# The passage from the FFN's up products to its down products: h loaded by quarters, the first down additions placed between the last pair's pieces

## What is computed

```
a, bb = jnp.split(u2 @ w_gate_upffn[i], 2, axis=-1)      # up: width 1024 -> 2 x 2816
h = h + (jax.nn.silu(a) * bb) @ w_down[i]                # down: 2816 -> 1024, added to h
```

## Time and profile before

| | before |
|---|---|
| median of 3 runs | 1698.7 us (1698.27 to 1705.17) |
| the profiled execution's own time | 1701.96 us |
| its span in the trace | 1700.2 us |
| PE busy | 1642.6 us, 97% of the span |
| DVE, POOL, ACT busy | 1157.0, 710.7, 624.9 us |
| bytes moved by DMA | 190.24 MB, mean 112 GB/s |

### The profile page before, as it was taken

How to read it: one execution, slowest core, us unless ns; L and a number is a source line. 1 busy time by engine, 2 the same in 40 slices (tenths; PEclk the granted TensorE clock), 3 DMA queues, 4 the chain that set the end, 5 groups by cost and what they waited for, 6 DMA issues and landing times.

```text
span 1700.2 us, 21565 instructions
## 1 busy us (share of the span) xinstructions
PE 1642.6 (97%) x7810; PEld 1353.8 (80%) x7810; DVE 1157.0 (68%) x1689; ACT 624.9 (37%) x978; POOL 710.7 (42%) x388
## 2 busy tenths in 40 slices
PE   9999999999999999999998999999989999989996
PEld 6888887887877888888886888878768888889785
DVE  7241799962498777777768666887948982585457
ACT  5031233421254444444443222264551111277114
POOL 2434111154514233223326687743465554443451
PEclk9999999999999999999999999999999999999998
DMA  5511100122523443344368976142101111100102
GB/s 192 84 45 42 36 27 29 35 102 109 185 88 125 174 155 141 144 163 152 146 229 311 408 311 260 70 155 58 36 25 50 49 49 38 63 26 1 37 26 99
DMA packets 52421, 190.24 MB, mean 112 GB/s; under 512 B 5681, under 2 KB 7618, under 8 KB 51562
## 3 DMA queue, kind: packets, MB, share of 16 engines
q1 hardware_dynamic: 47362, 171.61, 27.9%
q10 hardware_dynamic: 4968, 17.44, 3.5%
HBM read 133.97 MB, written 55.05 MB: 111 GB/s over the span
## 4 chain that ended last, share of the span: by engine, by line
PE 76%; DVE 12%; DMA 5%; issue 3%; ACT 2%; POOL 1%; ACTq 0%; POOLq 0%; SPq 0%; DVEq 0%
PE G L753 30%; PE U L996 10%; PE G L996 10%; PE U L1034 6%; PE G L1034 6%; PE G L1070 4%; DMA bias_scratch<-fvec 3%; PE U L1244 2%; PE U L899 1%; PE G L1231 1%; DMA h<-in_x_t 1%; DVE B_lo L1880 1%; DVE qt L1953 1%; DMA hid_spill<-hst 1%; DVE X_lo L2147 1%
## 5 line engine op out<-in xcount | busy, mean ns | idle before, releaser
L583 POOL TENSOR_SCALAR w_hi<-raw 128x1024 fp32r<-128x1024 f32 x50 | 149.6, 2991 | 295.1 <-PE G L753 217.8
L753 PE MATMUL G<-B_hi,w_hi 128*128 128x512 f32 x512 | 160.7, 395 | 5.0 <-DVE B_lo L1880 2.3
L753 PE MATMUL G<-B_lo,w_hi 128*128 128x512 f32 x512 | 158.4, 391 | 0.0
L753 PE MATMUL G<-B_hi,w_lo 128*128 128x512 f32 x512 | 158.0, 390 | 0.0
L753 PE MATMUL G<-A_hi,w_hi 128*128 128x512 f32 x448 | 144.3, 403 | 0.0
L621 POOL TENSOR_TENSOR S<-fraw 128x512 f32<-128x512 f32 x33 | 46.6, 1412 | 227.4 <-DVE ring_lo L2152 196.1
L753 PE MATMUL G<-A_lo,w_hi 128*128 128x512 f32 x448 | 138.9, 391 | 0.0
L753 PE MATMUL G<-A_hi,w_lo 128*128 128x512 f32 x448 | 138.3, 390 | 0.0
L585 POOL TENSOR_TENSOR w_lo<-raw,w_hi 128x1024 fp32r<-128x1024 f32 x50 | 132.2, 2645 | 4.2
L996 PE MATMUL G<-X_hi,ring_hi 128*128 128x512 f32 x308 | 120.7, 392 | 5.0 <-DVE X_lo L2147 2.9
L1469 ACT ACTIVATE ring_hi<-S 128x512 fp32r<-128x512 f32 x132 | 82.2, 628 | 110.2 <-PE U L1034 61.4
(11 more groups left out here) (393 smaller groups left out, 3841.2 us busy)
## 6 DMA issues: line engine op xcount, KB each, us to landing
raw<-in_weights SPq DMA_DIRECT2D x72, 512.0 KB, 3.6
hid_spill<-hst SPq DMA_DIRECT2D x72, 512.0 KB, 2.6
fraw<-in_weights SPq DMA_DIRECT2D x66, 512.0 KB, 4.5
Dc<-hid_spill SPq DMA_DIRECT2D x56, 512.0 KB, 12.5
Dc<-hid_spill ACTq DMA_DIRECT2D x14, 512.0 KB, 8.2
h<-in_x_t SPq DMA_DIRECT2D x8, 512.0 KB, 7.6
h<-in_x_t ACTq DMA_DIRECT2D x1, 4096.0 KB, 14.1
h_spill<-h SPq DMA_DIRECT2D x8, 512.0 KB, 6.7
```

The costliest lines, as they stand in the source:

```text
L583: pool.tensor_scalar(hi, raw[:, u, :], 1.0, None, ALU.mult).then_inc(w_hi_done, 1)
L753: mm = pe.matmul(G[g][:, b * HT:(b + 1) * HT], w, x[:, k, b * HT:(b + 1) * HT], start=s0, stop=s1)
```

## The change

1. **h by quarters.** `h_in(j)` becomes `h_in(j, *quarters)`. A quarter (a, n) is the tiles 4j + a and 4j + 2 + a, columns of half n: 512 KB in runs of 2 KB, where the whole load had runs of 16 KB. Each half of h has three semaphores: for (0, 0), for (1, 1), and one for (0, 1) and (1, 0) together. `down_add` waits for them at r = 0, 2 and 4 of the first two steps.
2. **SP's order.** The quarter (0, 0) of tiles 0 to 3 is issued after the first gated quarter of the last pair, (1, 1) after the second, the other two after the fourth. The quarter (0, 0) of tiles 4 to 7 is issued after the last pair's third piece, the other three after its seventh.
3. **DVE's order.** The additions of the first down step, which came after all four `turn_h`, with three of the pieces between them, are placed among the `turn_h` and the pieces: r = 0 after the first `turn_h`, r = 1 after the first piece, and so on.
4. **ACT's order.** The roundings of the weights UP + 1, r = 0 to 3, come after the fourth of the last pair's seven `hidden_hi` instead of after the seventh.

```diff
@@ SP
-            def h_in(j):
-                sp.dma_start(h[:, 4 * j:4 * j + 4, :].rearrange("p k n -> p (k n)"),
-                             h_spill[:, 4 * j * T:4 * (j + 1) * T]).then_inc(h_back[j], 16)
+            def h_in(j, *quarters):
+
+                for a, n in quarters:
+                    e = (0, 2, 1)[a + n]
+                    src = h_spill[:, 4 * j * T:4 * (j + 1) * T].rearrange("p (m a n) -> p m a n", m=2, a=2)
+                    dst = h[:, 4 * j:4 * j + 4, :].rearrange("p (m a) n -> p m a n", m=2)
+                    sp.dma_start(dst[:, :, a, hs(n)], src[:, :, a, hs(n)]).then_inc(h_back[j][e], 16)
...
+            sp.wait_ge(h_out, 16 * KT)
+            sp.wait_ge(hm_done, 4 * (GROUPS - 1) + 1)
+            h_in(0, (0, 0))
+            sp.wait_ge(hm_done, 4 * (GROUPS - 1) + 2)
+            h_in(0, (1, 1))
             sp.wait_ge(hm_done, 4 * GROUPS)
-            sp.wait_ge(h_out, 16 * KT)
-            h_in(0)
+            h_in(0, (0, 1), (1, 0))
             last += NR
-            for j in range(NR):
+            for j in range(3):
                 hidden_out(last + j)
-            for u in range(2):
-                sp.wait_ge(hs_out[u], 16 * (last // 2 + 1))
-            h_in(1)
+            sp.wait_ge(hs_out[0], 16 * (last // 2 + 1))
+            h_in(1, (0, 0))
+            for j in range(3, NR):
+                hidden_out(last + j)
+            sp.wait_ge(hs_out[1], 16 * (last // 2 + 1))
+            h_in(1, (1, 1), (0, 1), (1, 0))
             raw_in(UP + 2)
@@ ACT
-            for j in range(NR):
+            for j in range(4):
+                hidden_hi(last + j)
+            for r in range(4):
+                weights_hi(UP + 1, r)
+            for j in range(4, NR):
                 hidden_hi(last + j)
             for w in range(UP, LAST):
-                for r in range(NR):
+                for r in range(4 if w == UP else 0, NR):
                     weights_hi(w + 1, r)
@@ DVE
+                if d < 2 and r in (0, 2, 4):
+                    dve.wait_ge(h_back[d][r // 2], 32 if r == 4 else 16)
...
-            turn_h(last, 0), hidden_lo(NR * last), turn_h(last, 1), hidden_lo(NR * last + 1), turn_h(last, 2)
-            hidden_lo(NR * last + 2), hidden_lo(NR * last + 3), turn_h(last, 3)
-            dve.wait_ge(h_back[0], 16)
-            for r in range(NR):
+
+            def first_down(r):
                 down_add(r, 0, UP, 0, 0)
-                if r < 3:
-                    hidden_lo(NR * last + 4 + r)
-            dve.wait_ge(h_back[1], 16)
+            turn_h(last, 0), first_down(0)
+            hidden_lo(NR * last), first_down(1)
+            turn_h(last, 1), first_down(2)
+            hidden_lo(NR * last + 1), first_down(3)
+            turn_h(last, 2), hidden_lo(NR * last + 2), hidden_lo(NR * last + 3)
+            first_down(4)
+            turn_h(last, 3)
+            for j in range(4, NR):
+                hidden_lo(NR * last + j)
+            first_down(5), first_down(6)
```

More of the change, by code:

```diff
@@ L357, in build @@
         ch_in = [tile_in[0:NR], [sem(f"ch_in1_{r}") for r in range(NR)]]
-        h_back = [sem(f"h_back{j}") for j in range(2)]
+        h_back = [[sem(f"h_back{j}_{e}") for e in range(3)] for j in range(2)]
         dn_mid, dn_ev = sem("dn_mid"), [sem(f"dn_ev{m}") for m in range(2)]
```

## The result

| | before | after |
|---|---|---|
| median | 1698.2 us (1695.77 to 1705.17, 20 runs) | 1702.24 us (1698.29 to 1706.49, 20 runs) |
| ratio | | 1.0018, 95% interval 1.0009 to 1.0026: 3.1 us slower (1.5 to 4.4); the two medians differ by 4.0 |
| span of the profiled execution | 1700.2 us | 1697.8 us |
| PE's first down product starts | 909.16 us | 904.89 us |
| the stretch (below) | 85.05 us | 86.94 us |

The account below looks back on a forecast made before the run. PE, busy 97% of the span, was taken as the bound. Its 8.9 us stall goes, but the stream, 4.3 us late, starts step 4 3.0 us later: 1698.7 + 3.0 = 1701.7 us, range 1695.0 to 1706.0.

Parts of the forecast that it names:

- PE's stall at step 0: First down step, PE waiting for DVE's addition to h: 5.96 us plus 2.92 of slow clock, 8.9 us to win.
- the weights' stream: Saturated DMA transfers from about 933 to 1007 us: 4.3 us later than before, bounds 2.2 and 6.2.
- the slack: Start of down step 4: before the change, its weights' low part is ready 1.25 us ahead of PE's need.
- DVE's count: DVE's order in the first down step: 1.70 us per difference or piece beside POOL, 1.2 per pair of additions.
- the wait of 3.1 us at the start of step 1: PE waits 3.1 us for DVE's addition of r = 4, from 928.2 to 931.3.
- the slow clock behind it: After PE's earlier waits: a clock loss there only makes a later wait shorter.
- the forecast wait at step 3: Start of down step 3: PE ready at 973.9, low part at 976.8, a wait of 2.9 us.
- The estimate that I drew from it: DVE's last pieces: if each waits for one POOL operation, the seventh ends near 936, time 1.4 us above forecast.
- The seventh piece: Last of DVE's pieces, gating SP's later transfers: ends at 934.6 instead of 930.7, bounds 932.5 and 936.5.
- Two edits priced at nothing: ACT's earlier roundings of UP + 1: gain 0, bounds 0 to 1 us; early quarters of tiles 0 to 3: no gain.
- The gain did not arrive: Rival: the stream does not hold step 4, PE keeps 5.8 us, time 1692.9; chance 0.13.
- it did not even out: Rival: seventh piece ends before 932, stream late by no more than 1.25 us, time 1698.7; chance 0.12.
- the quarters did not run at half rate: Rival: quarters of tiles 4 to 7 hold DMA twice as long, 3.5 us on top, up to 1707.2; chance 0.05.

Follow-up runs that it names:

- the dose: Four extra 512 KB memory-to-memory copies issued ahead of the weights UP + 2: ratio to before 1.0049 in the changed kernel, 1.0026 in the kernel before.
- small_late: Changed kernel with ACT's three small loads for the second block (644 KB) issued two steps later; ratio to the kernel before 1.0010.
- h1_whole: Changed kernel with h of tiles 4 to 7 loaded in one 2 MB transfer behind the seventh piece instead of quarters; ratio to before 1.0017.
- wf_old_act: The kernel where the stream has been cleared, with ACT's order of the kernel before; ratio to the kernel before 0.9981.
- the kernel where the stream has been cleared: Changed kernel with weights UP + 2 to UP + 4 issued earlier by SP and ACT's three small loads later; ratio to the kernel before 0.9939.
- weights_first: Changed kernel with SP's order alone altered, weights UP + 2, UP + 3 and UP + 4 issued earlier; ratio to the kernel before 0.9978.
- wfsl_h0_late: The kernel where the stream has been cleared, with all quarters of h for tiles 0 to 3 issued behind the fourth gated quarter; ratio to before 0.9980.
- before_dose: Kernel before with four extra 512 KB copies between h of tiles 4 to 7 and the weights UP + 2; ratio to before 1.0026.
- before_weights_first: Kernel before with SP's order alone altered, weights UP + 2, UP + 3 and UP + 4 issued earlier; ratio to before 1.0006.
- before_wf_small_late: Kernel before with weights UP + 2 to UP + 4 issued earlier and ACT's small loads later, without the change; ratio to before 1.0002.
- quarters_only: Quarters of h and SP's order of the change, with DVE's and ACT's orders of the kernel before; ratio to before 0.9992.

## Why the prediction was right, and where its steps were off

*The result.* 3.0 us slower forecast, 3.1 (1.5 to 4.4) measured, for the reason given: PE's stall at step 0 goes, and what PE wins is given back to the weights' stream. That this is the cause is shown from four sides: the dose moves the stretch by about its own length in after, and by its length less the slack in before; taking bytes out shortens it; putting the weights ahead brings the gain out; and the same edits do nothing without the change. That the number was met so closely is luck in part: the stream was less late than forecast, 1.9 us of stretch instead of 3.0, and what brings the median back to 3.1 is, by my reading below, the varying slow clock of before, which the forecast did not have.

*The stream.* Forecast 4.3 us late (2.2 to 6.2), found 3.1 to 3.4. Step 4 starts 1.9 us later in the stretch, forecast 3.0. The slack of 1.25 us was right to a tenth or two (3.1 - 1.25 = 1.85). The median's 3.1 is more than the stretch's 1.9, but the stretch of before moves by 1.6 with its slow clock. In after, by my reading, a slow clock falls into a wait that swallows it. By the 83.5 to 85.1 seen for that order the change costs 1.9 to 3.5.

*The step that failed: DVE's count.* I took 1.70 for each difference and piece beside POOL. Where an addition stood ahead of them they took 0.60. The trace of before had shown it, in the piece at 928.19 beside this operation of POOL, and in the one at 929.98:

```profile
928.19 0.68 DVE L2192 TENSOR_TENSOR hst_last<-cb,hst_last 128x512 fp32r<-128x512 f32 x1
```

```profile
928.17 1.84 POOL L637 TENSOR_TENSOR ring_lo<-fraw,ring_hi 128x512 fp32r<-128x512 f32 x1
```

I had looked at the idle POOL of 924.59 alone. (The additions at 925.19 and 925.79, which I named as standing beside a busy POOL, stand beside an idle one too; the three in 1.87 us from 931.78 are the ones that show it.)

So in after the third addition of r = 4 ended 18.9 us into the stretch instead of 22.1, and the wait of 3.1 us at the start of step 1 that I had in the sum is not there (a few tenths are). Nor did it matter: PE reached step 2 2.4 us sooner and waited 5.7 there instead of 4.4, and the slow clock behind it, which I had allowed for, took the place of the forecast wait at step 3. The Trainium skill, "SBUF — State Buffer", section "Who interferes with whom", says that of two such instructions one blocks the other. The 1.7 agrees. The estimate that I drew from it, that each piece pays for a POOL operation, does not hold: behind an addition the pieces paid nothing, and POOL's operations, 1.84 us instead of 1.29, did.

*The seventh piece.* Forecast 25.4 us into the stretch (23.3 to 27.3), found 23.1, just below my lower bound (23.1 in small_late too, 23.9 in four other traces with the same orders of DVE and ACT). By my own formula the stream would then be 2.0 us late. It is 3.1. About 1 us stays without a proven name. At 930 to 936 the share is full at 309 to 323 GB/s, while the quarters and ACT's small loads run together; h1_whole puts some 0.7 us on the quarters, and the small loads, 644 KB that my list of the stream lacked, have moved ahead of UP + 2's weights. By wf_old_act the lateness of the seventh piece itself, 1.6 us against before, is more likely the price of ACT's edit than of the additions that I had counted; a run that takes this edit out of the changed kernel alone would tell.

*Two edits priced at nothing.* ACT's order and the early quarters are worth 4.2 and 3.6 us in the kernel where the stream has been cleared. "DVE holds the step until 931.3 anyway" was the cover that I named for ACT's, and it was not there: DVE's third addition ended 18.9 us into the stretch, in time for step 1. In the changed kernel PE waits 5.7 us at step 2 for the stream, which would hide both; that they are worth nothing there is argued from this wait and no run shows it, and ACT's edit may even cost there what it adds to the seventh piece.

*The rivals.* The gain did not arrive, it did not even out, and the quarters did not run at half rate (h1_whole).

## What to carry to other kernels

Before you remove an engine's stall, count what comes behind it from the memory side: each start of a step needs its last transfer, and the smallest slack there is all that a removed stall can win, less what the change itself delays those transfers. Here 8.9 us of stall stood against a slack of 1.25 and a stream that came 3.1 later. What brought the gain out was three pairs of transfers moved up in their queue, and three small loads moved out of the full stretch. A tuned kernel's edits hide each other: test each in the version in which nothing else waits, or its price may read as zero, and don't take the price found there for the one it has elsewhere.

## What the runs showed of the hardware that I had not expected

- The granted clock fell to 0.55 and 0.50 behind waits of PE of 2.3 and 2.5 us (weights_first, wfsl_h0_late), not only behind those of 4 to 6. Waits of 1.0 and 1.1 us, and one of 2.04 us (before_dose, step 3), did not do it.
- The slow stretch behind nearly the same stall of 5.5 to 5.8 us ended after some 3.4 us in three traces (before_weights_first, before_dose, h1_whole) and after 5.8 to 6.1 us in three others (before, before_wf_small_late, quarters_only). No edit explains it.
- Queued transfers of 512 KB hold 401 to 417 GB/s for 60 us on end (939 to 1002 after), with SP's issues paced by the queue. Three loads on ACT's queue, 644 KB, are not beside that stream but in it: without them UP + 2's weights came 2.3 us sooner (small_late).
- A DVE operation with two SBUF inputs beside a busy POOL took 0.60 us behind an addition that reads PSUM, and 1.7 behind another operation of its own kind. In the first case POOL's operations took 1.84 us instead of 1.29.
